# The level products of a recurrent stage: one product per two blocks instead of one per block, from keys packed by ScalarE

## The reference

```
S_t = diag(f_t) S_{t-1} + k_t v_t^T ; o_t = S_t^T q_t
q, f, i, g = split(h @ w_in, 4)
fg = lb + (1 - lb) * sigmoid(f)          # k = 1 - fg, v = i
o = hgrn2(silu(q), 1 - fg, i, log(fg))
o = o * rsqrt(mean(o*o) + eps) * g_norm_w * silu(g)
mixer = o @ w_out
```

## Time and profile before

| | us |
|---|---|
| median of 3 runs | 2456.12 (2456.11 to 2456.84) |
| the profiled execution, its span | 2456.5 |

### The profile page before, as it was taken

How to read it: one execution, slowest core, us unless ns; L and a number is a source line. 1 busy time by engine, 2 the same in 40 slices (tenths; PEclk the granted TensorE clock), 3 DMA queues, 4 the chain that set the end, 5 groups by cost and what they waited for, 6 DMA issues and landing times.

```text
span 2456.5 us, 31236 instructions
## 1 busy us (share of the span) xinstructions
PE 2418.6 (98%) x11642; PEld 1974.2 (80%) x11642; DVE 1394.3 (57%) x2270; ACT 908.5 (37%) x1299; POOL 159.8 (7%) x171
## 2 busy tenths in 40 slices
PE   9999999999999999999999999999999999999998
PEld 8777888888777788888788887888888877888886
DVE  4676555433666555542366765766643665766643
ACT  4454322223666432222333332533321564433312
POOL 0000000000000000000020000000030451000031
PEclk9999999999999999999999999999999999999999
DMA  4112222223122233222311112222223312322232
GB/s 173 61 60 78 95 94 94 86 94 103 61 69 69 86 97 100 94 77 94 122 68 68 51 68 95 86 94 94 93 87 106 135 53 78 103 94 94 85 112 94
DMA packets 61078, 218.93 MB, mean 89 GB/s; under 512 B 6805, under 2 KB 7349, under 8 KB 60864
## 3 DMA queue, kind: packets, MB, share of 16 engines
q1 hardware_dynamic: 58464, 208.28, 25.5%
q0 software_dynamic: 2064, 8.97, 1.0%
q10 hardware_dynamic: 464, 0.48, 0.1%
HBM read 215.59 MB, written 2.12 MB: 89 GB/s over the span
## 4 chain that ended last, share of the span: by engine, by line
PE 88%; DVE 6%; ACT 4%; issue 1%; DMA 0%; DVEq 0%; SPq 0%; ACTq 0%
PE ps L261 25%; PE ps L263 25%; PE ps L262 25%; PE ps L2001 2%; DVE stick_left L1386 1%; PE ps L1063 1%; DVE stick_p L1392 1%; PE ps L300 1%; PE ps L301 1%; ACT window_p L1667 1%; PE ps L305 1%; PE ps L1190 1%; PE ps L1051 1%; PE ps L1210 1%; PE ps L1077 1%
## 5 line engine op out<-in xcount | busy, mean ns | idle before, releaser
L261 PE MATMUL ps<-xh,wh 128*128 128x512 f32 x1832 | 729.3, 398 | 3.9 <-DVE wl L255 2.1
L263 PE MATMUL ps<-xh,wl 128*128 128x512 f32 x1832 | 715.1, 390 | 0.0
L262 PE MATMUL ps<-xl,wh 128*128 128x512 f32 x1832 | 714.2, 390 | 0.0
L247 ACT ACTIVATE wh<-raw 128x1024 fp32r<-128x1024 f32 x331 | 347.8, 1055 | 507.4 <-PE ps L263 470.8
L255 DVE TENSOR_TENSOR wl<-raw,wh 128x1024 fp32r<-128x1024 f32 x331 | 408.1, 1234 | 200.2 <-ACT wh L247 198.4
L261 PEld LDWEIGHTS ps<-xh,wh 128*128 128x128 f32 x1832 | 344.8, 188 | 77.8 <-issue 6.5
L263 PEld LDWEIGHTS ps<-xh,wl 128*128 128x128 f32 x1832 | 344.5, 188 | 73.1
L262 PEld LDWEIGHTS ps<-xl,wh 128*128 128x128 f32 x1832 | 345.0, 188 | 70.4 <-issue 2.2
L261 PE MATMUL ps<-wh,up_ah 128*128 128x512 f32 x528 | 205.7, 390 | 1.1 <-DVE wl L428 1.1
L262 PE MATMUL ps<-wl,up_ah 128*128 128x512 f32 x528 | 205.4, 389 | 0.0
L263 PE MATMUL ps<-wh,up_al 128*128 128x512 f32 x528 | 205.4, 389 | 0.0
(11 more groups left out here) (300 smaller groups left out, 3307.8 us busy)
## 6 DMA issues: line engine op xcount, KB each, us to landing
raw<-weights SPq DMA_DIRECT2D x387, 512.0 KB, 3.5
cst<-rows_d POOLq DMA_DIRECT2D x9, 512.0 KB, 4.8
hgrn_mask<-levels POOLq DMA_DIRECT2D x1, 2048.0 KB, 7.8
window_bias<-bias_rows POOLq DMA_DIRECT2D x1, 2048.0 KB, 9.4
hT<-x_t SPq DMA_DIRECT2D x7, 256.0 KB, 6.4
out_t<-hT SPq DMA_DIRECT2D x7, 256.0 KB, 2.1
cst<-consts SPq DMA_DIRECT2D x1, 832.0 KB, 8.9
raw<-weights SPq DMA_DIRECT2D x2, 256.0 KB, 4.1
```

The lines of the kernel that those rows point to most:

```text
L247: act.activation(wh[slot][:, :], raw[slot][:, :], ACT.Copy).then_inc(hi_done, 1)
L261: pe.matmul(out, w_hi, m_hi, start=first, stop=False, **kw)
L262: pe.matmul(out, w_hi, m_lo, start=False, stop=False, **kw)
L263: return pe.matmul(out, w_lo, m_hi, start=False, stop=last, **kw)
```

## The change

- The tokens are stored in the block order 0, 2, 1, 3, with blocks 1 and 3 backwards (`PLACE`, `stored`). The transposes write them so. The output is put back in order at the gating, which becomes two instructions of 256 columns instead of one of 512, into a new tile `normed`.
- In this storage the earlier keys of a pair of blocks (0 and 1, or 2 and 3) are 64 + 64. ACT copies them at each level into a tile `keys` (`act_pack`, 128 x 256, two tiles in turn), and a level product is two matmuls of 128 keys and 128 queries instead of four of 128 and 64. The entries between the two blocks are masked out: the mask has 256 columns per level, and is 1.15 MB instead of 2 MB.
- On DVE the keys of a level come first and the queries second. The keys wait for the pack of that level and not for the product, the queries wait for the product.
- Level 7 no longer has a form of its own.
- The low part of the third slab is made in two halves, after picks 5 and 6, instead of whole after pick 4.

```diff
+        def earlier(ap, m):
+            return across(ap, 0, [PAIR_COLS + m, 2], [2 * m, P // m], [1, m])
+        def earlier_keys(ap, m):
+            return across(ap, 0, [2 * m, P // m], [PAIR_COLS + m, 2], [1, m])
+        def later_queries(ap, m, pair):
+            return across(ap, pair * P + m, [PAIR_COLS - m, 2], [2 * m, P // (2 * m)], [1, m])
         def pe_product(pe, g, j, l, tail):
...
                 pe.wait_ge(g.uq_done, 8 * j + l - 1)
+            if 1 <= l < 8:
+                pe.wait_ge(g.packed, 7 * j + l)
+            elif l:
                 pe.wait_ge(g.uk_done, 8 * j + l - 1)
...
-                        n = 64 if l == 7 else P
-                        mm = pe.matmul(ps[0:n, p, b * 64:(b + 1) * 64], g.KG[:, at][:, 0:n],
-                                       halves(g.QF[:, at], 1 << (l - 1), 1), start=True, stop=True)
+            elif l < 8:
+                m = 1 << (l - 1)
+                out = ps[:, p, 0:PAIR_COLS].rearrange("p (e q c m) -> p e q c m", e=2, q=2, m=m)
+                for pair in range(2):
+                    mm = pe.matmul(out[:, :, pair, :, :], g.keys[p][:, token_block(pair)],
+                                   later_queries(g.QF[:, :], m, pair), start=True, stop=True)
...
+        def act_pack(act, g, j, l):
+            if l == 1:
+                act.wait_ge(g.start_ready, 2 * j + 1)
+            else:
+                act.wait_ge(g.uk_done, 8 * j + l - 1)
+            if l >= 3:
+                act.wait_ge(g.prod_done, 10 * j + l - 1)
+            m = 1 << (l - 1)
+            act.activation(g.keys[l % 2][:, :].rearrange("p (c e m) -> p c e m", e=2, m=m),
+                           earlier_keys(g.KG[:, :], m), ACT.Copy).then_inc(g.packed, 1)
...
             if not proj:
+                act_pack(act, g, j, 1)
                 split_hi(act, ph, HG - 1, 6)
+                act_pack(act, g, j, 2)
+                act_pack(act, g, j, 3)
                 split_hi(act, ph, HG - 1, 7)
+                for l in range(4, 8):
+                    act_pack(act, g, j, l)
...
-            dve.tensor_tensor(q2, q2, spread(left, m), ALU.mult).then_inc(g.uq_done, 1)
-            k1 = halves(g.KG[:, :], m, 0)
-            dve.tensor_tensor(k1, k1, spread(right, m), ALU.mult).then_inc(g.uk_done, 1)
+            dve.tensor_tensor(k1, k1, right, ALU.mult).then_inc(g.uk_done, 1)
+            dve.wait_ge(g.prod_done, 10 * j + l + 1)
+            dve.tensor_tensor(q2, q2, left, ALU.mult).then_inc(g.uq_done, 1)
...
-                    dve.tensor_tensor(g.og[:, :], g.og[:, :], g.rs[:, :], ALU.mult).then_inc(g.gated, 1)
+                out = g.normed[:, :].rearrange("p (q e t) -> p e q t", e=2, q=2)
+                dve.tensor_tensor(out[:, 0, :, :], og[:, 0, :, :], scale[:, 0, :, :], ALU.mult)
+                dve.tensor_tensor(out[:, 1, :, ::-1], og[:, 1, :, :], scale[:, 1, :, :], ALU.mult).then_inc(g.gated, 1)
...
-                return pe.transpose(ps[:, o.banks[j], b * P:(b + 1) * P],
+                return pe.transpose(o.leaves(ps[:, o.banks[j], :], b),
```

More of the change, by code:

```diff
@@ L64 @@
 LEVELS = 8
+PAIR_COLS = 2 * P
+MASK_COLS = S + (LEVELS - 1) * PAIR_COLS
+PLACE = [0, 2, 1, 3]
 class Phase:
@@ L1939, in __init__ @@
                 a = Arena("hgrn")
-                self.mask = a("mask", [P, LEVELS, S], I32)
+                self.mask = a("mask", [P, MASK_COLS], I32)
                 self.oh, self.ol = a("oh", [P, KT, S], F32R), a("ol", [P, KT, S], F32R)
@@ L2018, in pe_hgrn_values @@
             pe.wait_ge(g.G_ready, i)
-            off = {0: [(0, P, P), (2 * P, 2 * P, 2 * P)], 1: [(4 * P, 2 * P, 2 * P)], 2: [(P, 3 * P, P)], 3: []}
+            out = ps[:, 4, :]
+            off = {0: [(out[:, place(1)], 0, P), (last_two(out), 2 * P, 2 * P)], 1: [(last_two(out), 4 * P, 2 * P)],
+                   2: [(out[:, place(3)], P, P)], 3: []}
             for b in range(SB):
-                s = token_block(b)
-                mm = pe.matmul(ps[:, 4, s], g.v[:, s], g.sd[:, b, :], start=b == 0, stop=b == SB - 1,
+                s = place(b)
+                mm = pe.matmul(out[:, s], g.v[:, s], g.sd[:, PLACE[b], :], start=b == 0, stop=b == SB - 1,
                                skip_group_check=True)
-                for at, t, n in off[b]:
-                    pe.matmul(ps[:, 4, t:t + n], g.v[:, s], g.far[:, at:at + n], start=False, stop=False,
+                for to, at, n in off[b]:
+                    pe.matmul(to, g.v[:, s], g.far[:, at:at + n], start=False, stop=False,
                               skip_group_check=True)
@@ L2099, in act_head @@
             first = ph.first
+            if attn and proj:
+                for l in range(1, 5):
+                    act_pack(act, g, j, l)
             if proj:
@@ L2143, in dve_level @@
                 dve.wait_ge(g.ut_done, 7 * j + l - 1)
-            left, right = totals(g, m)
-            q2 = halves(g.QF[:, :], m, 1)
-            dve.tensor_tensor(q2, q2, spread(left, m), ALU.mult).then_inc(g.uq_done, 1)
-            k1 = halves(g.KG[:, :], m, 0)
-            dve.tensor_tensor(k1, k1, spread(right, m), ALU.mult).then_inc(g.uk_done, 1)
+            if l == 1:
+                dve.wait_ge(g.prod_done, 10 * j + 1)
+            if l < 8:
+                dve.wait_ge(g.packed, 7 * j + l)
+            else:
+                dve.wait_ge(g.prod_done, 10 * j + 9)
+            if m < P:
+                left, right = earlier_totals(g, m), later_totals(g, m)
+                q2, k1 = later(g.QF[:, :], m), earlier(g.KG[:, :], m)
+            else:
+                t, at = total_at(g, m)
+                left, right = (across(t, at + n, [1, 2], [0, m]) for n in (0, 2))
+                q2, k1 = (ap.rearrange("p (b m) -> p b m", m=m) for ap in (g.QF[:, PAIR_COLS:], g.KG[:, 0:PAIR_COLS]))
+            dve.tensor_tensor(k1, k1, right, ALU.mult).then_inc(g.uk_done, 1)
+            dve.wait_ge(g.prod_done, 10 * j + l + 1)
+            dve.tensor_tensor(q2, q2, left, ALU.mult).then_inc(g.uq_done, 1)
         def dve_pick(dve, g, j, l):
@@ L2263, in hgrn_pool @@
             pool.memset(g.sd[:, :, :], 0.0).then_inc(g.cleared, 1)
-            pool.dma_start(g.mask[:, :, :], levels).then_inc(g.masks_in, 16)
+            pool.dma_start(g.mask[:, :], levels).then_inc(g.masks_in, 16)
             between()
@@ L2543, in constants @@
     put("sin", np.sin(angle.astype(np.float64)).astype(np.float32)[row] * sign[:, None])
-    one = np.zeros((P, LEVELS, P), np.int32)
-    one[:, 0, :] = np.eye(P)
+    levels = np.zeros((P, MASK_COLS), np.int32)
+    levels[:, 0:S] = np.tile(np.eye(P), (1, SB))
     for l in range(1, LEVELS):
-        m = 1 << (l - 1)
-        left = (q // m) % 2 == 0
-        one[:, l, :] = left[:, None] & (q[None, :] // m == (q // m)[:, None] + 1)
-    levels = np.tile(one, (1, 1, SB))
+        m, at = 1 << (l - 1), S + (l - 1) * PAIR_COLS
+        here = levels[:, at:at + PAIR_COLS].reshape(P, 2, 2, P // (2 * m), m)
+        for e in range(2):
+            for c in range(P // (2 * m)):
+                first = (2 * c + e) * m
+                here[first:first + m, e, :, c, :] = 1
     hot = np.zeros((BUCKETS + 1, 3 * WINDOW), np.float32)
```

95 lines of the change are left out of this document (61 added, 34 removed).

## The result

The changed kernel takes 2434.78 us (median of 4 runs, 2432.59 to 2435.52), the kernel before 2456.48 beside it (2456.11 to 2459.49). The ratio is 0.9907, 95% interval 0.9896 to 0.9919. The forecast was 2435.4. The profiled execution of the changed kernel has a span of 2433.2 us.

The account below looks back on a forecast made before the run. PE's stream was taken to bound the recurrent stage (34.14 us a head). Gains of 15.4 (heads 1 to 6), 3.2 (head 0) and 2.1 (head 7), sum 20.7, took 2456.5 to 2435.8, median 2435.4 us; 8-in-10 range 2431 to 2445.

Parts of the forecast that it names:

- The level product, 0.45 us less: Products 1 to 7 on PE: 4 loads with 128 columns instead of 8 loads, spacing 2.28 to 1.83 us.
- matmuls with gaps stream at half rate: Rival, level products: spacing 2.23, total 2454.6 us, chance 0.05; at the two finest levels alone 2441.8, chance 0.06.
- The path of a level, hidden by 0.8 to 1.1 us: ACT's pack in a level: ready 2.6 to 2.9 us after a load, wanted at 3.66, so hidden.
- Product 2, wait 0.62: Product 2 in the loop: PE ready at 1325.73, pack at 1326.35, so PE waits 0.62 us, 0.17 later than before.
- The third slab, 0.05: Third projection: low part's second half ready at 2.44 us, wanted at 2.40; a wait of 0.04, charged as 0.05.
- The loop head, 2.56: Heads 1 to 6, load of product 0 to product 8: 18.30 us becomes 15.69, less 0.05 for the slab; gain 2.56 each.
- Head 7, 2.1: Last head, behind the loop: 13.5 us to product 8 becomes 11.13, less 0.17 and 0.08; gain 2.1 us.
- the 0.15 for pack 4: Head 7: 0.15 us charged since pack 4 stands behind a high part that waits for PE until 1500.7.
- Backwards transposes and mask, 0: Transposes writing PSUM backwards: taken as 0, +1.7 us if they double; smaller mask, loaded long before use: 0.
- That the new order doesn't hold PE: Rival, larger gain: product 2 comes 0.45 to 0.6 us sooner in 7 heads, 2431.5 us; chance 0.06.
- DVE as the bound: Rival, levels on DVE: each of three operations costs 0.63 us instead of 0.33, total 2472 us; chance 0.04.
- the signs of being wrong: Profile after: level spacings above 1.9 us, DVE multiplications above 0.45, or a third-projection wait of more than 0.3.

Follow-up runs that it names:

- the four-matmul variant: Changed kernel with each level product as four matmuls of 64 queries from the same packed keys, same order: 2457.09 us, ratio 1.0003 to the kernel before.
- the last kernel: Changed kernel with the output split moved behind picks 1 and 2 of the next head, last head's first-slab low part halved: 2432.59 us, second run 2430.91.

## Why the prediction was right

*The level product, 0.45 us less.* Right: spacing 1.82 to 1.84, and the four-matmul variant is back at the old time (stage 270.81 against 270.64). The rival that matmuls with gaps stream at half rate is out: a spacing of 2.23 would have shown, and half the columns changed nothing. The Trainium skill (Advanced Engine Details and Errata, Memory Cachelines) says that two hits on a 16-byte line of SBUF are enough. Level 1, at 1.84 in head 0 as the other levels, agrees; since the columns don't set the time here, a somewhat slower read could have stayed hidden, so this doesn't prove it.

*The path of a level, hidden by 0.8 to 1.1 us.* Right in kind: doubling packs 3 to 7 costs nothing in the loop. Two sizes were off. The pack lasts 0.42 and not 0.38 (0.52 at level 1, 0.45 at level 2). DVE takes up a product after 0.86 us, not 0.96. The 0.96 had been read at product 8 of the kernel before; in the changed kernel product 8 is taken up after 1332.87 - 1332.00 = 0.87, and why is open.

*Product 2, wait 0.62.* Measured 0.64 to 0.67 in heads 1 to 6 and none in head 0, and 2.45 behind product 1 against 2.44. The pack was 0.07 longer than charged, and the handovers around it 0.05 shorter (0.03 and 0.06 instead of 0.07 twice). What I missed is that a product that waits isn't loaded early, and the next comes 0.1 us sooner (1.73) from load to load, so the wait costs some 0.5 us and not 0.62.

*The third slab, 0.05.* No wait: DVE's 0.86 instead of 0.96 left 1330.73 - 1330.65 = 0.08 us. The margin is as thin as forecast, and the whole low part after pick 4 would have cost 3.2 us.

*The loop head, 2.56.* Measured 2.75. The difference is these three: 0.10 behind the wait, 0.05 at the slab, and 0.05 from five spacings of 1.82.

*Head 7, 2.1.* Measured 2.32. Product 4's load began 0.1 us late behind pack 4 (1482.94), but its matmuls began 1483.06 - 1481.24 = 1.82 behind those of product 3, so the 0.15 for pack 4 wasn't paid, and 0.1 came back behind the wait. From product 8 on the head took 12.56 us instead of 12.45, 0.11 for the 0.08 charged; 0.07 of it show as the longer wait for `hgrn_ol`, 0.76 us instead of 0.69.

*Backwards transposes and mask, 0.* Right for the transposes, by a run of their own. The mask had none; its transfer ends at 1220.3 + 5.2 = 1225.5 us, and the first pick that reads it starts at 1255.5.

*The rivals.* That the new order doesn't hold PE: wrong, its load waited 0.64 to 0.67 us in heads 1 to 6, and in head 7, where it had waited before, product 2 came 0.19 later still; the 4.5 us that this and the tail cost were then gained by moving the output split. DVE as the bound: no. Of the level products' picks two are slow, as before. One of the signs of being wrong did appear, DVE multiplications above 0.45 us, at two of the seven levels, and it cost PE nothing (see the end).

The end, 2435.4 against 2434.78, is closer than the terms were, and that is luck. The stage gave 22.0 us where the sum said 20.7; 0.3 of it are not in the medians, and the kernel before was 0.36 slower in the measurement beside the changed kernel (2456.48) than in the one that the forecast started from (2456.12).

## What to carry to other kernels

When halving the columns of a group of small matmuls changes nothing, count its load and matmul pairs and merge products, even with half of the output masked out. Here 4 pairs cost 0.91 us with 128 columns and 1.31 with 256, and 1.83 from product to product with 64 as with 128. A producer put in between (the pack) was hidden here because the step that it waits for comes first on its engine, and cost 13.4 us where it came second; look for the one place where its input is late for another reason, and move what can wait behind it. Where full times scatter by more than the effect, compare one stage between two marks: here that was good to 0.2 us, while full times of the changed kernel spread over 4 to 5 us in its two repeats.

## What was not expected of the hardware

- A matmul group that has waited for its operands is followed 0.1 us sooner by the next one (1.73 against 1.82 to 1.84 us), and its result is taken up 0.76 us after its load began instead of 0.86. So taking away a wait of 0.65 gains 0.5. This is a matter of where one counts from, and nothing runs faster: the load of such a group starts only 0.03 us ahead of its matmuls (1321.17, 1321.20), that of another 0.22 (1322.90, 1323.12). From matmul to matmul the next group comes 1323.12 - 1321.20 = 1.92 us later, not 1.82. The early load that is lost costs 0.1.
- ACT's copy of 256 fp32 columns lasts 0.52 us when it picks every second element, 0.45 with runs of 2, and 0.42 with longer runs, against 0.38 for the contiguous copy from PSUM in the earlier trace rows. Whether the last step is the gaps or the other source isn't shown.
- DVE's multiplications don't depend on such runs: 0.41 to 0.44 us, but 0.45 to 0.48 for the keys of levels 2 and 3, which follow right behind a pick of 0.72. Where the output split stands between, in heads 1 to 7 of the last kernel, these last 0.43 at most.
- PE's transposes write PSUM backwards in the time that they take forwards, 1.09 us for 8 of 128 fp32 columns.
